# Modulation chunks as column-tiled fp32 matmuls, and the differential attention rebuilt on 64-row score tiles

## The reference

```python
ml = jnp.split((c_act @ w_mod[i] + b_mod[i])[:, None, :], 6, axis=-1)
mc = jnp.split(cc_act @ w_mod[i] + b_mod[i], 6, axis=-1)

def diff_attn_core(q, k, v, lam):            # q: 8 heads x 2 halves of 64
    s = jnp.einsum('bhiqd,bhikd->bhiqk', q, k).astype(jnp.float32) * (q.shape[-1] ** -0.5)
    p = jax.nn.softmax(s, axis=-1)
    a = (p[:, :, 0] - lam * p[:, :, 1]).astype(v.dtype)
    return jnp.einsum('bhqk,bhkd->bhqd', a, v)

def head_out(o):
    o = rms_norm(o, subln_g, SUBLN_EPS) * (1.0 - lam_init)
    return o.reshape(o.shape[0], o.shape[1], DIFF_V_WIDTH) @ w_out
```

## Time and profile before

| | |
|---|---|
| median of 3 runs | 1827.17 us (1825.93 to 1829.61) |
| the profiled execution | 1823.06 us, its span 1821.3 us |
| mean TensorE clock | 0.962 of full |
| TensorE busy | 1672.1 us, 92% |
| VectorE busy | 1136.6 us, 62% |
| ScalarE busy | 559.1 us, 31% |
| GpSimd busy | 637.5 us, 35% |

### The profile page before, as it was taken

How to read it: one execution, slowest core, us unless ns; L and a number is a source line. 1 busy time by engine, 2 the same in 40 slices (tenths; PEclk the granted TensorE clock), 3 DMA queues, 4 the chain that set the end, 5 groups by cost and what they waited for, 6 DMA issues and landing times.

```text
span 1821.3 us, 23734 instructions
## 1 busy us (share of the span) xinstructions
PE 1672.1 (92%) x8978; PEld 1386.1 (76%) x8978; DVE 1136.6 (62%) x1485; ACT 559.1 (31%) x953; POOL 637.5 (35%) x344
## 2 busy tenths in 40 slices
PE   7789989988799999999999899977778899999997
PEld 2667878877688888888888787866664788888886
DVE  2877408687896887897542668058885471616173
ACT  3311337414111111111122311278884331212121
POOL 1522256224222322323322524243321464444341
PEclk9899999998899999999999899989999999999998
DMA  8334221440242234234111223100010232232321
GB/s 327 106 121 158 93 76 37 148 143 23 99 162 99 92 136 141 93 105 149 59 69 35 82 68 95 47 1 0 1 36 0 81 105 93 94 102 92 92 92 47
DMA packets 56395, 163.86 MB, mean 90 GB/s; under 512 B 7144, under 2 KB 7400, under 8 KB 54768
## 3 DMA queue, kind: packets, MB, share of 16 engines
q1 hardware_dynamic: 56304, 162.68, 26.6%
HBM read 159.77 MB, written 2.10 MB: 89 GB/s over the span
## 4 chain that ended last, share of the span: by engine, by line
PE 69%; DVE 16%; ACT 6%; issue 5%; POOL 2%; DMA 1%; SPq 0%; DVEq 0%; ACTq 0%; POOLq 0%
PE ps L1435 20%; PE ps L1436 20%; PE ps L1437 20%; DVE mod_acc L1027 8%; ACT aprob L957 2%; ACT at_hi L943 1%; PE ps L1708 1%; PE ps L1698 1%; POOL h_lo L532 1%; DMA mod_big<-w_mod_dram 1%; PE ps L1736 1%; DVE tmp_b L1165 1%; PE ps L1587 1%; DVE h_hi L1142 1%; PE ps L1479 1%
## 5 line engine op out<-in xcount | busy, mean ns | idle before, releaser
L521 POOL TENSOR_TENSOR w_lo<-raw,w_hi 128x1024 fp32r<-128x1024 f32 x189 | 471.9, 2500 | 922.4 <-ACT w_hi L664 922.3
L1435 PE MATMUL ps<-h_lo,w_hi 128*128 128x512 f32 (+1 forms) x1152 | 415.6, 361 | 24.3 <-DVE h_lo L1145 12.9
L1436 PE MATMUL ps<-h_hi,w_lo 128*128 128x512 f32 (+1 forms) x1152 | 412.4, 358 | 0.0
L1437 PE MATMUL ps<-h_hi,w_hi 128*128 128x512 f32 (+1 forms) x1152 | 409.2, 355 | 0.0
L664 ACT ACTIVATE w_hi<-raw 128x1024 fp32r<-128x1024 f32 x189 | 199.4, 1057 | 419.5 <-PE ps L1437 408.1
L1436 PE MATMUL ps<-hid_hi,w_lo 128*128 128x512 f32 (+1 forms) x784 | 276.7, 353 | 0.0
L1435 PE MATMUL ps<-hid_lo,w_hi 128*128 128x512 f32 (+1 forms) x784 | 276.5, 353 | 0.0
L1437 PE MATMUL ps<-hid_hi,w_hi 128*128 128x512 f32 (+1 forms) x784 | 274.9, 351 | 0.0
L1027 DVE SCALAR_TENSOR_TENSOR mod_acc<-mod_ring,cact,mod_acc 128x512 f32<-128x512 f32 x280 | 256.8, 958 | 28.4 <-DVE mod_acc L1027 23.4
L1435 PEld LDWEIGHTS ps<-h_lo,w_hi 128*128 128x128 f32 x1152 | 221.8, 193 | 61.9 <-issue 15.8
L1436 PEld LDWEIGHTS ps<-h_hi,w_lo 128*128 128x128 f32 x1152 | 221.7, 192 | 31.7 <-issue 1.5
(11 more groups left out here) (198 smaller groups left out, 2450.2 us busy)
## 6 DMA issues: line engine op xcount, KB each, us to landing
raw<-units_dram SPq DMA_DIRECT2D x189, 512.0 KB, 3.7
mod_ring<-w_mod_dram SPq DMA_DIRECT2D x160, 256.0 KB, 2.8
mod_big<-w_mod_dram SPq DMA_DIRECT2D x8, 1024.0 KB, 12.1
xl<-x_dram SPq DMA_DIRECT2D x2, 2048.0 KB, 11.9
bias<-bias_dram SPq DMA_DIRECT2D x8, 384.0 KB, 3.6
xc<-ctx_dram SPq DMA_DIRECT2D x2, 1024.0 KB, 13.9
out_dram<-out_t SPq DMA_DIRECT2D x8, 256.0 KB, 2.9
v0s<-v SPq DMA_DIRECT2D x6, 128.0 KB, 2.9
```

Source lines behind the costliest of these rows:

```text
L521: nc.gpsimd.tensor_tensor(w_lo[:, s], raw[:, s], w_hi[:, s].bitcast(F32), op=ALU.subtract).then_inc(lo_made, 1)
L1435: mm(out, a[0], b[1], start=start, stop=False)
L1436: mm(out, a[1], b[0], start=False, stop=False)
L1437: return mm(out, a[0], b[0], start=False, stop=stop)
```

## The change

- Chunks 0 to 11 of the modulation (PE_MODS = 12) all go over TensorE. The stationary operand is widened to 32 columns (`cact_wide`, zeros beyond the first two), and k = 0..3 and then 4..7 go to the four groups of 32 PSUM partitions, so that the four groups hold four partial sums. ScalarE copies all 128 partitions, and the turn is a matmul of the copy with `group_sum` [128, 2], which adds the four groups.
- Chunks 4 to 11 are loaded as two 1 MB halves each into slots that follow each other (the third of `mod_big`, and `mod_late`); `half_mm` stands behind units 3 to 10, `half_turn` behind units 4 to 11. `mix_mods`, `out_mods` and their steps, sums and extracts are gone. Chunks 12 to 23 stay on VectorE.
- Attention 1: queries and keys are split as whole 128-row tiles (`aqh`, `aql`, `akh`, `akl`). Scores are three products of 64 rows for each half, the two halves side by side in the array, in three pairs of banks taken in turn. The first half is no longer divided by its sum: the combine is e1 + (lam * l1 / l2) * e2, and the sub-norm gets epsilon times l1 squared instead (`eps_terms`, and four small matmuls with `ident` per group in `sub_sums`). The transposes go in two threes through bank 6 and are copied as fp32 (`turned1`), and `weigh1` is one fp32 matmul of `v1` with `aturn` per block, in bank 7. Gone are ScalarE's scaling and swaps, VectorE's low parts of keys and probabilities, and GpSimd's split of the values. GpSimd makes `aqh`, `aql`, `akl`; ScalarE `akh`.

```diff
@@ TensorE, modulation
-                for k in range(KT):
-                    if k % 4 == 0:
-                        pe.wait_ge(big_in[m % 3][k // 4], 16 * (m // 3 + 1))
-                    ins = mm(ps[0:2, m % 2], cact[:, k], big[:, m % 3, k], start=k == 0, stop=k == KT - 1)
+                i, target = mod_slot(m)
+                for j in range(2):
+                    pe.wait_ge(big_in[i][j], target)
+                    for g in range(4):
+                        k = 4 * j + g
+                        ins = mm(ps[32 * g:32 * g + 32, mod_banks(m)[0]], cact_wide[:, k], mod_w[i][:, k],
+                                 start=j == 0, stop=j == 1)
...
-                if i == 2:
-                    mod_mm(4)
-                elif i >= 4 and i % 2 == 0:
-                    pe.wait_ge(mod_done, 3 + i // 2)
-                    mod_mm(3 + i // 2)
+                if 4 <= i < PE_MODS:
+                    half_turn(i)
+                if 3 <= i < PE_MODS - 1:
+                    half_mm(i + 1)
@@ SyncE
-            for m, k in mix_mods(-1):
-                load_mod(m, k)
+            sp.wait_ge(half_summed, 3)
+            load_half_mod(4)
             sp.wait_ge(h_made, KT)
             sp.dma_start(dft_raw[:], t["dft128"]).then_inc(table_in, 16)
+            load_half_mod(5)
 
             for u in range(FIRST["out0"]):
                 load_unit(u + SLOTS, u % SLOTS)
-                for m, k in (mix_mods(u - 1) if 1 <= u <= FIRST["dft"] else ()):
-                    load_mod(m, k)
+                if 6 <= u < PE_MODS:
+                    sp.wait_ge(half_summed, u - 1)
+                    load_half_mod(u)
@@ TensorE, attention 1
+            def scores1(n):
+                h, p = n // 4, n // 4 % 2
+                if n % 4 == 0:
+                    pe.wait_ge(jl1, h + 1)
+                    pe.wait_ge(kl1, h + 1)
+                if n >= 1:
+                    pe.wait_ge(e1, 2 * n - 1)
+                else:
+                    pe.wait_ge(v1_out, NT + 4)
+                tok = slice(P * (n % 4), P * (n % 4) + P)
+                for j, (a, b) in enumerate(((aql, akh), (aqh, akl), (aqh, akh))):
+                    for ks in (slice(0, LAT), slice(LAT, TOK)):
+                        for i in range(2):
+                            ins = mm(scores_ps(n, i)[:, ks], a[p][64 * i:64 * i + 64, tok], b[p][64 * i:64 * i + 64, ks],
+                                     start=j == 0, stop=j == 2)
+                            if j == 2 and ks.stop == TOK:
+                                ins.then_inc(s1, 1)
+            def turn1(n, j):
+                if j == 0:
+                    pe.wait_ge(a1, n + 1)
+                if n or j:
+                    pe.wait_ge(th1, 2 * n + j)
...
+            def weigh1(m):
+                h = m // 2
+                pe.wait_ge(th1, 4 * m + 4)
+                if m >= 1:
+                    pe.wait_ge(o1, m)
                 for c in range(NT):
+                    ins = mm(out_ps, v1[:, c, P * h:P * h + P], aturn[m % 2][:, c], start=c == 0, stop=c == NT - 1)
                 ins.then_inc(pv1, 1)
...
                 if 1 <= n <= N1:
-                    turn1(n - 1)
+                    turn1(n - 1, 0)
+                if n >= 4 and n % 2 == 0:
+                    weigh1((n - 4) // 2)
+                if 1 <= n <= N1:
+                    turn1(n - 1, 1)
@@ ScalarE, attention 1
             for n in range(N1 + 5):
                 h = n // 4
-                if 1 <= n <= N1:
-                    scale_second(n - 1)
-                if n < N1:
-                    exps(n, 0)
-                if 2 <= n <= N1 + 1:
-                    p_high1(n - 2)
-                if n < N1:
-                    exps(n, 1)
-                if h + 1 < HEADS and n % 4 < 2:
-                    keys_high1(h + 1, n % 4)
-                if h + 1 < HEADS and 1 <= n % 4 < 3:
-                    swaps1(h + 1, n % 4 - 1)
+                for i in range(2):
+                    if 2 <= n <= N1 + 1:
+                        turned1(n - 2, i)
+                    if n < N1:
+                        exps(n, i)
+                if h + 1 < HEADS and n % 4 == 1:
+                    keys_high1(h + 1)
@@ VectorE, attention 1
-            for n in range(N1 + 2):
+            for n in range(N1 + 1):
                 if n < N1:
                     least1(n)
-                if 1 <= n <= N1:
+                if n >= 1:
+                    ratio(n - 1)
                     combine(n - 1)
-                if n >= 2:
-                    p_low1(n - 2)
-                if n < N1:
-                    coef(n)
-                if n // 4 + 1 < HEADS and 1 <= n % 4 < 3:
-                    keys_low1(n // 4 + 1, n % 4 - 1)
```

More of the change, by code:

```diff
@@ L51 @@
 VARIANT = [0, 1, 1, 2]
-SPLIT_HALF = 10
+PE_MODS = 12
 RING = 4
[L56 to L68, removed]
 MOD_AT = [range(0, 4), range(4, 8), (), ()]
@@ L155, in build @@
         acc_hi = at("acc_hi", [P, 2, 512], F32R, mod_at + size(RING + 2, 512))
+        cact_wide = at("cact_wide", [P, KT, 32], F32, mod_at + size(2, 512))
         big = at("mod_big", [P, 3, KT, 512], F32, rest)
+        mod_late = at("mod_late", [P, KT, 512], F32, scr)
+        mod_w = [big[:, i] for i in range(3)] + [mod_late[:]]
         hid_hi = at("hid_hi", [P, KT, TOK], F32R, rest)
@@ L356, in build @@
         sub_lo = sem("sub_lo")
-        big_in = [[sem(f"big_in{i}{j}") for j in range(2)] for i in range(3)]
+        big_in = [[sem(f"big_in{i}{j}") for j in range(2)] for i in range(4)]
         shift_in = [sem(f"shift_in{j}") for j in range(3)]
@@ L422, in _ @@
                     sp.wait_ge(half_summed, 1)
-                for j in range(2):
-                    sl = slice(4 * j, 4 * j + 4)
-                    sp.dma_start(big[:, m % 3, sl], t["w_mod"][m][:, sl]).then_inc(big_in[m % 3][j], 16)
+                load_half_mod(m)
                 if m == 1:
@@ L928, in _ @@
                 else:
-                    act.wait_ge(unit_done, FIRST["v1"] + 5)
-                    for i in range(2):
-                        keys_high1(0, i)
-                        swaps1(0, i)
+                    act.wait_ge(unit_done, FIRST["v1"] + 6)
+                    keys_high1(0)
                 act.wait_ge(unit_done, FIRST["v1"] + 4 * j + 4)
@@ L1207, in mlp @@
                 blk(HID_BLOCKS - 1, True)
+            dve.sem_inc(mod_used, RING)
+            st.wait(V.memset(cact_wide[:], 0.0))
             st.wait(V.memset(mod_acc[:, 0, 0:P], 1.0))
@@ L1380, in _, with eps_terms @@
+                V.scalar_tensor_tensor(out=aprob[:, n % 3, 0], in0=aprob[:, n % 3, 1], scalar=stat[:, d:d + 1],
+                                       in1=aprob[:, n % 3, 0], op0=ALU.mult, op1=ALU.add).then_inc(a1, 1)
+            def eps_terms(n0, n1):
+                V.scalar_tensor_tensor(out=l_eps[:, n0:n1], in0=l_first[:, n0:n1], scalar=SUB_EPS * P,
+                                       in1=l_first[:, n0:n1], op0=ALU.mult, op1=ALU.mult).then_inc(leps_ok, 1)
             N1 = 4 * HEADS
-            for i in range(2):
-                keys_low1(0, i)
@@ new lines, in sub_sums @@
+                if h >= HEADS - 2:
+                    pe.wait_ge(leps_ok, 2 if last else 1)
+                    le = l_eps[:].rearrange("p (h t) -> p t h", t=4)
+                    for t_ in range(4):
+                        tok = slice(P * t_, P * t_ + P)
+                        if last:
+                            ins = mm(ps[0:1, 1, tok], le[:, t_, h:], ident[:], start=False, stop=t_ == 3)
+                        else:
+                            ins = mm(ps[0:HEADS - 1, 0, tok], le[:, t_, 0:HEADS - 1], ident[:], start=False, stop=t_ == 3)
+                    ins.then_inc(sub_mm, 1)
```

307 lines of the change are left out of this document (121 added, 186 removed).

## The result

The changed kernel takes 1777.16 us (median of 4 runs, 1774.24 to 1782.19) against 1826.55 for the kernel before on the same chip: a ratio of 0.973, 95% interval 0.9701 to 0.9758. The forecast was 1776. Its profiled execution took 1774.65, with a span of 1772.5 where the one before had 1821.3: 48.8 less, where the terms came to 50.8.

The account below looks back on a forecast made before the run. TensorE, busy 92%, was taken as the bound, with time winnable only where it waits or runs slowly. 11.2 + 4.0 + 9.6 + 26 = 50.8 off 1823.06 gives 1772.3; medians lie 4.1 higher, so 1776 us, range 1756 to 1800.

Parts of the forecast that it names:

- Start: Before the first projections: column-grouped chunks at 2.2 us each bring the first norm near 40.5, 8.5 us earlier.
- Projections: First projections: modulation sums moved to TensorE, small transforms start at 175.7 instead of 186.91, 11.2 us less, start included.
- The edge case: First projections: chunk 5's load goes ahead of unit 4's weights; if late, it costs 1 to 3 us.
- Rival 2: Modulation chunks: four column groups overlap only by two, 3.5 us a chunk, 10 us more, 1787; chance 0.13.
- Small transforms: After the first projections: without idle time, low clock and a sum, 10.1 us instead of 14.1, 4.0 less.
- Output projection: Output projection: idle time, modulation sums and low-clock work go, about 9.6 us less (8 to 10).
- Attention: Differential attention: loop 28 us less, first scores 1.0 later, end 1.0 more; net 26 us less.
- the walk: Attention loop, two tiles followed engine by engine: 8.4 us a pair, 9.2 with the key copy, 17.6 a head.
- Behind the last scores: End of attention: scaling and low parts go, weighing moves before the last sums, epsilon matmuls come; 1.0 us more.
- Rival 1: Attention loop: hand-overs hide, 3.9 to 4.05 us a tile, 12 us less, 1764; chance 0.15.
- Rival 3: Attention keeps part of its old pace (POOL's splits or half-overlapping 64-row pairs): 5.0 a tile, 19 us more, 1795; chance 0.11.
- Rival 4: Attention loop: TensorE at 1.2 GHz throughout, 81 us more, 1857; decides from about 62% at lower clock; chance 0.04.

## Why the prediction came out right, step by step

- *Start*, 8.5 forecast, 4.65 measured. The chunk's cost was right (1.92 against 2.2), its surroundings not. Context landed at 24.3, since xc's 17.1 us from issue were not in the reckoning, only x's 15.1; the norm sums ended at 35.8, ahead of chunk 3 in TensorE's queue; and TensorE, idle 7.27 us for loads, did both at its lower clock (3.40 for 1.92). Another 1.2 us are VectorE's two small products (1.66 for 0.49). The two reorderings show that this start is a knot of in-order queues: moving one thing forward moved the norm back by 3.6, twice.
- *Projections*, 175.7 forecast for the small transforms, 177.58 measured. From first projection to transforms 129.55 us against 131.5 in the sum: the cheaper chunks give back half of what the start missed. The edge case came as a wait of 0.70. *Rival 2* fails: a chunk takes 1.92 us, so the overlap is four-way, and the experiment in one column group shows that it is worth 48 us, as the rival's 47 for no overlap said.
- *Small transforms*, 10.1 forecast, 10.17 measured. *Output projection*, 9.6 forecast (its own terms add up to 9.8), 9.3 measured.
- *Attention*, 26 forecast. Measured are 26.7 from the first scores to output projection 1, or 25.7 with the 1.0 that the first scores wait longer, as forecast. That is close by luck, out of two errors that cancel. The loop gave 32.4 us where 28 was forecast: the old one was 169.5 from first to last scores, not 167.5, and the new one is 137.15, not 139. The head is 17.75 against 17.6, with a reason that is half wrong: the dear pair was laid to the key copy on ScalarE; that costs 0.4 (the 3.80), and the rest, 0.9 to 1.1, was VectorE's combination beside GpSimd's split, which the walk held hidden.
- *Behind the last scores*, 1.0 more was put down and 5.7 more measured. This is the term that failed, and it is TensorE's work, not its waiting: idle time in this part is 4.2 us, where it was 4.4. One weighing more stands behind the start of the last scores (2.6 us from start to next start), since in the new order a weighing stands behind a tile's scores and no longer ahead of them; the two groups of epsilon matmuls cost some 0.95 each by their starts; two weighings in fp32 are each 0.3 to 0.4 longer than three products were. That is 5.2 of the 5.7, and a mere sum of TensorE's work there would have shown it.
- *Rival 1*, a tighter loop at 3.9 to 4.05 us a tile, fails for the change as it is (4.4), but the room was there: with even weighing and a third buffer a tile takes 3.5 in the steady heads. The prediction's far end for the attention, "35 less", doesn't agree with this rival's own 12 us under the walk, which make 38. *Rival 3* fails: a head is 17.75. Its first reason, GpSimd's splits beside VectorE's instructions, was there all the same, at 6 us for the loop instead of 19. Its second, 64-row pairs that overlap half, was not: six pairs take 1.26 us. What it would have cost, the experiment shows in part: with 1.72 a tile the loop was 7.9 longer. *Rival 4* fails: 0.50 in the first head, 0.91 on the mean, where above 0.95 was looked for; far from the 62% at which it decides. *Rival 5* fails: the add ahead of the transforms cost 0.38.
- The change of tiling mode, which by the Trainium skill, "TensorEngine Tiling (Array Packing)", Key Properties, drains TensorE: six pairs take 1.26 us from the start of the scores to that of the turn, against 1.36 in the sum. No further 0.3 each way is to be seen.

## What to carry to other kernels

When an in-order pipeline of four engines has slack on each, write down for every tile which one is full and which waits: here tiles of 3.4 and 4.8 us took turns, and another order of TensorE's work with one more buffer was worth 24 us, half as much as the whole change. When such an edit gains, look at the other engines too: some 6 us of the 24, by the run with the split moved, came from a collision of VectorE and GpSimd that the new order happened to end. And check in the trace that an experiment did what it was to do: the scores one map after the other still overlapped. Before moving a load or an instruction forward, follow every queue that holds an instruction on what it makes later. Last, add up the work behind a loop as carefully as that inside it.

## What the runs showed of the hardware

- Four column groups of 32 with fp32 operands overlap nearly in full: 16 records in 1.92 us, against 7.05 in one group. The estimate of 2.9 us by the figure for three column tiles in the Trainium skill, "TensorE: Matmul & The Clock Gate", Part 3, was too high.
- VectorE's combination of two SBUF operands takes 2.13 us instead of 1.02 beside a GpSimd subtraction of 1.29 us, 1.72 beside a GpSimd square of 1.04 (once), while its minima over PSUM stay at 1.82 for two.
- Matmuls on two groups of 64 rows overlap even when they are not neighbours in the program: six on one group followed by six on the other take 1.72 us up to the turn instead of 1.26, and the seventh starts with the third.
- The granted clock over the first 56 us of output projection 1 is 0.82 in one kernel's trace, and 0.94 to 1.00 in the traces of eleven others; with 0.97 in the changed kernel, that is 7 us of time.
